# Low halves on VectorE beside the attentions, matmuls ahead of the first transposes, and bank 0 first at the feed-forward boundary

## What is computed

```python
# first block
proj = rms_norm(x, norm_g) @ w_in                      # 1024 x 3864
dq, dk, dv, dz, nq, nkv, nz, ng = split(proj)
o_diff = rms_norm(softmax(dq0 dk0) v - lam * softmax(dq1 dk1) v) * silu(dz)   # "diff", 4 heads
o_nsa  = (g0 * o_compressed + g1 * o_selected + g2 * o_window) * silu(nz)     # "nsa", 8 heads
x = x + concat(o_diff, o_nsa) @ w_out
# second block
proj = rms_norm_2(x, g_mix) @ w_in_2                   # 1024 x 4808
y_a  = short_conv_mixer(c_b, c_c, c_x) @ w_branch_a
y_b  = dsa_attention(q, k, v, top-k of index scores) @ w_branch_b             # "dsa", 8 heads
x = x + (sigmoid(g_a) * y_a + sigmoid(g_b) * y_b) @ w_out_2
h = rms_norm_2(x, g_ffn)
x = x + (silu(h @ w_ffn_gate) * (h @ w_ffn_up)) @ w_ffn_down                  # 1024 -> 2816 -> 1024
return rms_norm_2(x, g_final)
```

## Time and profile before

| what | us |
|---|---|
| median of 3 runs (1120.16 to 1125.7) | 1122.06 |
| the profiled execution | 1125.76 |
| its span | 1123.9 |
| PE busy | 1083.2 (96%) |
| PE weight loads busy | 848.8 (76%) |
| DVE busy | 452.0 (40%) |
| ACT busy | 442.3 (39%) |
| POOL busy | 527.6 (47%) |

### The profile page before, as it was taken

One profiled execution on the slowest core, in us unless ns is written; L12 is line 12 of the kernel. 1 busy time (PEld: TensorE's weight loads), 2 busy tenths in 40 slices (PEclk: granted clock), 3 DMA queues, 4 the chain that ended last, 5 costly groups with the idle time before them and its releaser, 6 DMA issues.

```text
span 1123.9 us, 14211 instructions
## 1 busy us (share of the span) xinstructions
PE 1083.2 (96%) x5380; PEld 848.8 (76%) x5380; DVE 452.0 (40%) x921; ACT 442.3 (39%) x771; POOL 527.6 (47%) x442
## 2 busy tenths in 40 slices
PE   6999999899998999999999999989999999999997
PEld 5888776555666886788867778878888888888886
DVE  4744587635443233795854225240000000023334
ACT  6333436466655343422355442441212122232532
POOL 3444541146457533335465434434354444546662
PEclk9999999899999999999999999999999999999999
DMA  9522321111013232132321222322323323232231
GB/s 297 162 89 53 97 76 38 38 38 39 1 38 109 80 86 91 41 113 81 107 76 38 76 73 78 113 75 75 112 75 112 94 93 109 78 113 64 105 113 75
DMA packets 83667, 96.08 MB, mean 85 GB/s; under 512 B 8089, under 2 KB 68722, under 8 KB 83610
## 3 DMA queue, kind: packets, MB, share of 16 engines
q1 hardware_dynamic: 83050, 93.20, 26.4%
q0 software_dynamic: 560, 2.12, 0.6%
HBM read 93.20 MB, written 2.12 MB: 85 GB/s over the span
## 4 chain that ended last, share of the span: by engine, by line
PE 92%; DVE 4%; issue 1%; ACT 1%; POOL 1%; DMA 0%; DVEq 0%; SPq 0%; ACTq 0%
PE bank L1576 54%; PE bank L1831 22%; PE bank L1612 4%; PE bank L1637 3%; PE bank L1674 3%; PE bank L1704 1%; PE bank L1653 1%; PE bank L1767 1%; PE bank L1591 1%; PE bank L1812 1%; DVE L L1280 1%; DVE h_lo L1500 0%; POOL w_lo L894 0%; DVE pool L1285 0%; DVE zs L1447 0%
## 5 line engine op out<-in xcount | busy, mean ns | idle before, releaser
L894 POOL TENSOR_TENSOR w_lo<-raw,w_hi 128x512 fp32r<-128x512 f32 x230 | 319.1, 1418 | 330.6 <-ACT w_hi L972 316.5
L1576 PE MATMUL bank<-h_hi,w_hi 128*128 128x512 f32 (+1 forms) x584 | 238.6, 409 | 2.9 <-DVE h_lo L1500 1.5
L1576 PE MATMUL bank<-h_hi,w_lo 128*128 128x512 f32 (+1 forms) x584 | 229.7, 393 | 0.0
L1576 PE MATMUL bank<-h_lo,w_hi 128*128 128x512 f32 (+1 forms) x584 | 229.5, 393 | 0.2 <-DVE h_lo L1492 0.2
L949 POOL TENSOR_TENSOR w_lo<-raw,w_hi 128x512 fp32r<-128x512 f32 x88 | 110.7, 1289 | 140.0 <-ACT w_hi L1175 73.0
L972 ACT ACTIVATE w_hi<-raw 128x2048 fp32r<-128x2048 f32 (+3 forms) x58 | 107.9, 1860 | 122.3 <-PE bank L1576 121.4
L1831 PE MATMUL bank<-h_hi,w_hi 128*128 128x512 f32 x352 | 138.5, 393 | 4.1 <-DVE h_lo L1500 4.1
L1831 PE MATMUL bank<-h_lo,w_hi 128*128 128x512 f32 x352 | 138.2, 393 | 0.0
L1831 PE MATMUL bank<-h_hi,w_lo 128*128 128x512 f32 x352 | 138.1, 392 | 0.0
L1576 PEld LDWEIGHTS bank<-h_hi,w_hi 128*128 128x128 f32 (+1 forms) x584 | 110.7, 189 | 32.5 <-issue 7.4
L1576 PE MATMUL bank<-w_hi,h_hi 128*128 128x512 f32 x336 | 131.5, 391 | 0.0
(11 more groups left out here) (177 smaller groups left out, 1295.9 us busy)
## 6 DMA issues: line engine op xcount, KB each, us to landing
raw<-in_w_in SPq DMA_DIRECT2D x30, 1024.0 KB, 5.4
raw<-in_w_ffn_gate SPq DMA_DIRECT2D x11, 1024.0 KB, 5.4
raw<-in_w_ffn_up SPq DMA_DIRECT2D x11, 1024.0 KB, 5.3
raw<-in_w_out SPq DMA_DIRECT2D x8, 1024.0 KB, 5.1
raw<-in_w_ffn_down SPq DMA_DIRECT2D x8, 1024.0 KB, 5.0
pool<-in_cmp_w SPq DMA_DIRECT2D x4, 1024.0 KB, 8.7
raw<-in_w_in SPq DMA_DIRECT2D x6, 512.0 KB, 5.4
raw<-in_w_ffn_down SPq DMA_DIRECT2D x4, 768.0 KB, 4.3
```

The lines of the kernel that those rows point to most:

```text
L894: nc.gpsimd.tensor_tensor(w_lo[:, u.n % 2, cols], raw[:, u.n % 2, cols], w_hi[:, u.n % 2, cols].bitcast(F32), ALU.subtract).then_inc(lo_do ...
L1576: ins = mm(bank[t.bank][0:t.m, :], stationary, moving, start=s and p == 0, stop=e and p == 2, skip_group_check=u.token)
```

## The change

- Each unit gets a semaphore for its low half, `lo_by`: `lo_dve` for nv, nz0, nz1, z0, z1 and gates 3 to 7, `lo_done` for all others. For the ten units POOL leaves the split out, and DVE makes the four subtractions as "low_piece" entries of the plan, one in each of the four slots that follow the split's slot. The first of them waits for ACT's high half of the unit. PE and SP wait on the semaphore of the unit.
- POOL's very first piece also waits until all rows of x are normed (`xn_done` = 5).
- PE makes 14 matmuls of the identity with itself, 128x128x128 in float32, into bank 4 right behind L1747. Nothing reads their result; the transposes overwrite the bank.
- `turn[RING4] = 0` ahead of the second output projection, so that its tiles take the banks 0, 1, 2, 3, 0, 1, 2, 3 in place of 3, 0, 1, 2, 3, 0, 1, 2. The last tile is then in bank 3 and not in bank 2, and the next bank of the ring is 0 and not 3.

```diff
--- before.py
+++ after.py
@@ -196,12 +196,14 @@
 
     order = (dq_u[:1] + [kv_u] + dk_u[:1] + dq_u[1:] + dk_u[1:] + nq_u + [ng_u, nk_u] + dv_u + [nv_u] + nz_u + z_u
              + out1_u + iq_u + [kik_u] + q_u + cb_u + cc_u + cx_u + gate_u + branch_u + out2_u + ffn_u + down_u)
-    ring_in, lo_pieces = [0, 0], 0
+    beside_attention = nv_u, *nz_u, *z_u, *gate_u[3:]
+    ring_in, lo_pieces = [0, 0], Counter()
     for n, u in enumerate(order):
         u.n = n
-        u.lo0 = lo_pieces
-        lo_pieces += -(-u.nk * u.width // PIECE)
-        u.lo_end = lo_pieces
+        u.lo_by = "lo_dve" if u in beside_attention else "lo_done"
+        u.lo0 = lo_pieces[u.lo_by]
+        lo_pieces[u.lo_by] += -(-u.nk * u.width // PIECE)
+        u.lo_end = lo_pieces[u.lo_by]
         u.hi0 = order[n - 1].hi_end if n else 0
         u.hi_end = u.hi0 + (1 if n else FIRST_PIECES)
         ring_in[n % 2] += 16 * (len(u.parts) if u.parts else 1)
@@ -305,6 +307,9 @@
                         before()
                     if not started and next_of[u.n] is not None:
                         emit("split", u=next_of[u.n], of=u)
+                        if next_of[u.n].lo_by == "lo_dve":
+                            for o in range(0, ND * 256, PIECE):
+                                later(1 + o // PIECE, lambda nxt=next_of[u.n], o=o: emit("low_piece", u=nxt, o=o))
                     started = True
                     ks = range(k, min(k + size, u.nk))
                     end = ks[-1] == u.nk - 1
@@ -561,6 +566,7 @@
     for m in range(4, ND):
         split_source("merged", m, "DVE")
     fresh[0] = "merged"
+    turn[RING4] = 0
     project(out2_u, RING4, 4)
     transposed_norm(R_FFN, banks_after(out2_u[-1].tiles[-1].bank, RING4))
 
@@ -710,6 +716,7 @@
         raw_in = [sem("raw_in0"), sem("raw_in1")]
 
         hi_done, lo_done, part_done, tile_done = sem("hi_done"), sem("lo_done"), sem("part_done"), sem("tile_done")
+        lo_dve = sem("lo_dve")
 
         sc_evac, ve_evac, res_done, branch_done = sem("sc_evac"), sem("ve_evac"), sem("res_done"), sem("branch_done")
 
@@ -749,7 +756,7 @@
 
         bias_dram = nc.dram_tensor("bias_dram", [DSA_HEADS, BIASW], F32, kind="Internal").ap()
 
                        branch_done=branch_done, aux_root=aux_root, aux_done=aux_done, aux_copied=aux_copied,
                        norm_done=norm_done, cmp_lg_done=cmp_lg_done, h_lo_done=h_lo_done, h_lo_pool=h_lo_pool,
                        h_hi_done=h_hi_done, col_done=col_done,
@@ -804,7 +811,7 @@
         def _(sp):
             def load(u):
                 if u.n >= 2:
-                    sp.wait_ge(lo_done, order[u.n - 2].lo_end)
+                    wait_free(sp, [(order[u.n - 2].lo_by, order[u.n - 2].lo_end)])
                 if u.n == 0:
                     src, half = u.parts[0][0], u.nk // 2
                     sp.dma_start(slot(raw, 0, u)[:, 0:half, :], src[:, 0:half, :]).then_inc(w0_in, 16)
@@ -890,6 +897,8 @@
                 size = u.nk * u.width
                 for o in range(0, size, PIECE):
                     pool_e.wait_ge(hi_done, u.hi0 + o // PIECE + 1 if u.n == 0 else u.hi_end)
+                    if u.n == 0 and o == 0:
+                        pool_e.wait_ge(xn_done, NT + 1)
                     cols = slice(o, min(o + PIECE, size))
                     nc.gpsimd.tensor_tensor(w_lo[:, u.n % 2, cols], raw[:, u.n % 2, cols],
                                             w_hi[:, u.n % 2, cols].bitcast(F32), ALU.subtract).then_inc(lo_done, 1)
@@ -915,7 +924,7 @@
             nc.gpsimd.memset(vc[:, :, :], 0.0).then_inc(zero_done, 1)
             split_lo(order[0])
             for kind, e in plan:
-                if kind == "split":
+                if kind == "split" and e["u"].lo_by == "lo_done":
                     split_lo(e["u"])
                 if kind == "small_arrays":
 
@@ -1463,6 +1472,11 @@
             for kind, e in plan:
                 if kind == "split" and e["of"].act and e["of"].act0 + 1 < len(down_u):
                     split_act_lo(down_u[e["of"].act0 + 1])
+                if kind == "low_piece":
+                    u, cols = e["u"], slice(e["o"], e["o"] + PIECE)
+                    ve.wait_ge(hi_done, u.hi_end)
+                    v.tensor_tensor(w_lo[:, u.n % 2, cols], raw[:, u.n % 2, cols], w_hi[:, u.n % 2, cols].bitcast(F32),
+                                    ALU.subtract).then_inc(lo_dve, 1)
                 if kind == "evacuate":
                     evacuate(e["t"])
                 if kind == "finish":
@@ -1559,7 +1573,7 @@
                     pe.wait_ge(a_lo_done, act_done_at(u, 0))
                 for k in ks:
                     if j == 0:
-                        pe.wait_ge(lo_done, u.lo0 + ((k + 1) * u.width - 1) // PIECE + 1)
+                        wait_free(pe, [(u.lo_by, u.lo0 + ((k + 1) * u.width - 1) // PIECE + 1)])
                     h = 4 * (u.act0 % 2) + k if u.act else u.k0 + k
                     if u.act and j == 0 and u.act0 == 0:
                         pe.wait_ge(a_lo_done, act_done_at(u, k))
@@ -1745,6 +1759,8 @@
 
             pe.wait_ge(first_in, 32)
             nc.tensor.transpose(bank[COL_BANK][:, 0:ND], vec_rows[0:ND, :], ident[0:ND, 0:ND]).then_inc(col_tr, 1)
+            for _ in range(14):
+                mm(bank[4][:, 0:P], ident, ident, start=True, stop=True)
             for kind, e in plan:
                 if kind == "matmuls":
                     matmuls(**e)
```

More of the change, by code:

```diff
@@ L750, in build @@
         bias_dram = nc.dram_tensor("bias_dram", [DSA_HEADS, BIASW], F32, kind="Internal").ap()
-        by_name = dict(aux_in=aux_in, ve_evac=ve_evac, sc_evac=sc_evac, hid_done=hid_done, res_done=res_done,
+        by_name = dict(lo_done=lo_done, lo_dve=lo_dve, aux_in=aux_in, ve_evac=ve_evac, sc_evac=sc_evac, hid_done=hid_done, res_done=res_done,
                        branch_done=branch_done, aux_root=aux_root, aux_done=aux_done, aux_copied=aux_copied,
```

## The result

| | before | after |
|---|---|---|
| runs, us | 1122.06, 1120.16, 1125.70, 1123.21 | 1111.95, 1111.21, 1108.92, 1111.17 |
| median | 1122.63 | 1111.19 |
| ratio, 95% interval | | 0.9893, 0.9865 to 0.9922 |
| profiled execution, its span | 1125.76, 1123.9 | 1111.95, 1110.2 |
| mean granted clock of it | 0.987 | 0.995 |

Forecast were 1112.2 and a range of 1107 to 1119. Between the two profiled executions there are 13.8 us, since that of before lies high among its runs.

The account below looks back on a forecast made before the run. PE holds 92% of the chain, so only its waits and slow clock can be won. -6.4 - 1.6 - 1.9 = -9.9 us from 1125.76 gives 1115.9, or 1112.2 from the median 1122.06; range 1107 to 1119.

Parts of the forecast that it names:

- Bank 0 first: Feed-forward boundary: PE starts after one h_lo instead of six and keeps its clock; -6.4 us, range 2.0 to 6.6 gained.
- Rival 1: Feed-forward boundary: the clock falls all the same, gain there only 2.0 us, total 1116.6; chance 0.08.
- The row before the second block: Before the second block, the same transposes are followed by matmuls at 0.230 us from the first on; evidence for -6.4.
- The start: Kernel start: 14 matmuls raise PE's clock, POOL's gate shortens the second half row; -1.6 us, from -2.0 to +1.0.
- rival 5: Start: 14 matmuls don't raise the clock; +2.6, total 1114.8, inside the forecast's own range, no separate chance.
- The low halves: Attentions and gates: low halves moved from POOL to DVE; units sum to -1.9 us, bounds -5 and +6.
- nv: L1415 and its twin shrink, -2.0; two pieces cost +1.5, two more +0.7; net +0.2 us.
- nz0: Scores at 177.92: three pieces ahead of logits cost 2.2 us, less some 1.5 of swelling; +0.7.
- nz1: Near 202 to 208.87 us: next scores 1.2 later, the awaited copy about 1.1 earlier; net -1.1 us.
- rival 4: At 208 us the shorter wait lets PE keep its clock, some 3 us more gained, total 1109.2; chance 0.09.
- Rival 2: Attentions: DVE pieces collide with POOL's scalings (3.7 us on PE's path), z0's 2.3 not hidden; +6.0, total 1118.2; chance 0.14.
- part 3: The prediction's part on moving low halves to DVE, a piece costing 0.73 us; sum -1.9 us.
- Rival 3: First two attentions: DVE becomes the bound if a piece costs over 0.93 us; total 1133.4; chance 0.03.

Follow-up runs that it names:

- short pieces: The whole change, but DVE's low pieces of nv, nz and z 4 columns wide in place of 512: 1106.85 us, -15.5 against the kernel before.
- the kernel whose two profiles have no fall before the last 5 us: The whole change with DVE's low pieces of nv, nz and z two slots later: 1108.49 us, in the repeat 1107.93 against 1111.01 for the whole change.

## Why the prediction was right, and where it was not

The time was 1111.2 for a forecast of 1112.2, inside the range, and faster by over 0.5%. Two of the three parts were mis-sized, in opposite directions, and together the parts gave less than the sum of what each gives alone; that the total came within 1 us is in part luck. The mechanisms hold by the traces, except for what is said of the start.

**Bank 0 first: right.** Forecast -6.4 (3.4 of waiting, 3.0 of clock); traces 3.25 and 1.3 to 2.8 (2.2 in the mean of the seven executions of the old ring), runs -7.5 alone and -5.7 within the whole. Rival 1, a clock that falls there anyway, fell: 0 of 7. The row before the second block was the right evidence for it. The up weights' low half was not late: PE waits once in the boundary, 0.89 us, and for h_lo.

**The start: one half of the mechanism was right, the size was not.** Forecast -1.6; on average 0.75 at the first large matmul, -1.2 (-2.9 to +0.3) alone, nothing within the whole. The step that failed is the one that set the cold 5.61 us of the earlier trace rows as what the kernel before always does. In four of the six executions without the 14 matmuls it is so, in two the clock rose during the transposes by itself and the first large matmul came at 13.9 to 14.0. The sum had the two edits need each other; the second half row does shrink from 1.52 to 0.48 as forecast, but the matmuls alone bring the first large matmul to 14.02 (one execution) and GpSimd's wait alone leaves it at 15.17, so that the wait's part is not shown. The matmuls did raise the clock, so rival 5 falls. In after a transfer that landed at 8.48 was late next, which the sum did not have.

**The low halves: waits forecast -1.9, -3.6 in the table and -2.8 once nz0 is put right, and 4.5 of clock on top.** By unit, forecast and table:
- nv +0.2, measured -0.35: the swelling that goes away is the -2.0 of the forecast (L1415 and its twin take 0.68 each in the kernel without the start), but the two pairs of pieces cost 1.2 and 0.4 where it had 1.5 and 0.7.
- nz0 +0.7, measured -0.03 in the table, which sets a fall of the clock at 167 us in the kernel before against none. Over eleven executions (table above) the stretch takes 10.7 to 10.9 with DVE's pieces, whether the clock falls or not, and 10.6 to 10.8 or 9.1 without them. So the pieces cost 0.1 where the clock falls and 1.6 where it holds, 0.7 in the mean of what was seen.
- nz1 -1.1, measured +1.33 and -2.72, together -1.4. Both halves were forecast (+1.2, and the copy earlier), and the wait of 3.64 went to 0.94.
- z0 0, measured +1.70 and -1.66: the later logits are taken in by the wait for the compressed keys' values, as forecast.
- z1 -1.3, measured -1.32, and PE no longer waits for POOL's scalings.
- gates -0.4, measured -0.5.

What was outside the sum is the clock. Around 208 us PE's waits before were 0.59 and 3.64 close together, and the matmuls behind ran at the lower of the two levels, in 5 of 5 executions. In the six executions whose waits there are 1.92 to 1.94 and at most 0.94 the clock fell in three, and earlier, at 202 to 204 us, where it cost 0.5 to 1.1 us; in the three with short or later pieces (0.59 or 1.44, then 0.92 or 0.94) it did not fall there. Behind the copy the stretch is 2.9 us shorter than in the kernel before where the clock holds. That is rival 4, which had 9%, and it came true in full in half of these executions and for the larger part in the others. A second fall, at 235 to 243 us, followed in 4 of 5 old executions and in none of the nine with DVE's pieces, 1.6 us, and I had no rival for that. That the shorter waits are what keeps the clock up is read off these counts; no run changes the waits and nothing else. Both should have weighed more: the prediction itself read the boundary's clock off a wait of 4 us, and used the same reasoning at 208 us only for a rival.

**Rival 2, collisions and waits on DVE, +6.** Its parts are there, in small. The Trainium skill, SBUF — State Buffer, "Who interferes with whom", says that a DVE instruction with two SBUF inputs contends with a GpSimd instruction that reads SBUF. The trace agrees in both directions: with POOL's pieces gone from the first attention DVE's L1341 at 128x512 went from 979 to 752 ns in the mean and L1358 from 355 to 285, and with DVE's pieces beside the second and third attention POOL's own scalings grew (below; before they took 445, 631 and 827 ns). Three quarters of the growth is in the third: there the forms of 128, 256 and 384 columns go from 433, 612 and 827 ns to 580, 795 and 1046, and they stay at 444, 615 and 828 in the kernel that leaves the gates' low halves on POOL. In the second, where the rival had its collisions, the same forms go from 452, 640 and 827 to 498, 640 and 880. The 80, 61 and 108 ns on 24 scalings of a form are 6 us of POOL time in all, and PE waits for none of it, where the rival had put half of its collisions on PE's path. How long one of the two engines holds the ports, no run here shows. The rival's +6.0 is counted from the forecast; as a bound of the sum of part 3, where the prediction also puts it, it would be +4.1.

```profile
L912 POOL TENSOR_TENSOR L<-L,st 128x384 f32<-128x384 f32 x24 | 22.0, 935 | 39.1 <-DVE st L1355 23.0 <-DVE st L1357 16.1
L912 POOL TENSOR_TENSOR L<-L,st 128x256 f32<-128x256 f32 x24 | 16.1, 692 | 30.2 <-DVE st L1357 15.8 <-DVE st L1355 14.4
L912 POOL TENSOR_TENSOR L<-L,st 128x128 f32<-128x128 f32 x24 | 12.1, 525 | 106.0 <-DVE st L1355 89.1 <-DVE st L1357 16.8
```

**Rival 3, slower.** It needed a piece above 0.93 us; the mean is 0.71. The short pieces show that length matters, but by some tenths at each wait, 2.5 us at most in all, not 19.

**What stays open.** Alone, the three parts give 7.5, 1.2 and 7.0 us, 15.7 together; the whole gives 12.1. The intervals of the three leave room for that. The falls of the clock at 340 and 430 us, 1.3 to 1.6 each, which two of the three executions of the change with and without its start part have each and the low halves alone has not, would account for some 2 us, but no run shows what causes them. Nor is it shown why the clock stays up in the kernel with the pieces two slots later, or what brings the falls around 165 and 340 us.

## What to carry over

Where one engine holds nine tenths of the chain, a wait of a few microseconds on it has two prices, its length and the matmuls at half clock behind it; cost both wherever the profile shows a lower granted clock right behind a wait. Work moved onto an engine that others wait for should stand in its order where its own input is ready: here pieces two slots later did the same work and gave 3.1 us more, 2.2 of it in shorter waits. Ask of each buffer order which tile the next stage needs first: bank 0 first is one line, and half of the gain.

## What the runs showed of the hardware

- The scatter of the kernel before goes with the clock. Twelve runs with GpSimd's wait alone, a kernel that times like the one before, run from 1119.2 us at a mean granted clock of 0.994 to 1126.0 at 0.987; the whole change has a scatter of 3.0 us in eight runs (1108.92 to 1111.95, clock 0.993 to 0.998), the kernel whose two profiles have no fall before the last 5 us ran from 1106.4 at 0.998 to 1111.0 at 0.995.
- One and the same cold start can go two ways: 28 transposes in 4.60 us (0.164 each) in one execution and 32 in 6.50 (0.203) in another, with the same instructions ahead of them.
- A fall of the clock can take back a gain made elsewhere: between the same two matmuls (352.77 and 461.50 before) the executions with a fall at 430 us take 108.7 to 108.9 us and those without 107.2 or 107.3, whatever had been gained ahead of it (one, whose fall at 340 us reaches into this stretch, 108.1).
- Where PE waits for other engines anyway, a fall costs little. With DVE's pieces it costs 0.2 us at 167 us, where PE waits 1.17 and 0.95 us for logits if the clock holds and 0.83 once if it falls, and 0.5 to 1.1 us at 203 us; with POOL's pieces it costs 1.6 at 167 and 1.6 at 235 us.
